# Two routing passes of a fused transformer kernel, each gathered into one stage on unnormalised tokens

## The chip, the cores and the metric

The kernel runs on one core of a Trainium2 chip. The metric is the device time of one execution in microseconds (us), lower is better. The core's engines are TensorE (PE, with its weight loads as PEld), VectorE (DVE), ScalarE (ACT), GpSimd (POOL) and the queue of SyncE (SP), which issues the transfers from HBM.

## The reference, cut to what matters

A sequence of 256 tokens with 1024 features passes through a first block (attention, a gated unit, cross attention, a mixture of experts) and through a second block of two layers, the last of which ends in another mixture. Everything is float32. Each mixture first normalises the tokens, then routes:

```
y = x * rsqrt(mean(x*x) + 1e-6) * g                 # g: one factor for each of the 1024 columns
# first mixture: 4 groups of 4 experts
glog = y @ w_rg + b_rg ; elog = y @ w_re + b_re     # 4 and 16 logits for each token
# best group by glog; best two experts of that group by elog; softmax over the two, times the group's probability
# second mixture: 8 experts
logits = y @ router                                  # best two, softmax over the two
# both: x += sum over the chosen experts of weight * (silu(y @ w_gate) * (y @ w_up)) @ w_down
```

## The kernel before

The program is a chain of stages. A stage is a block in which every engine has a program of its own, and no engine goes on to the next stage before all have ended. Weights come as pieces of 512 KB through a ring of 12 raw slots (`ring`). ScalarE writes the high part of a piece (`ring_hi`, L403, in the type float32r) and VectorE the low part (`ring_lo`, L408). SyncE loads a new piece into a slot when the piece that lay there has its low part. Each stage lets SyncE issue what fits (`issue_loads`).

The tokens `x` stand as rows, 128 on the partitions, in two halves (`[128, 2, 1024]`). `xT` is a pair (high, low) of turned tokens, `[128, 8, 256]`, with features on the partitions. Before each mixture these stages run:

- `clear_routing` (L2509 to L2517) loads the column factors as a row (`gain_row`) and clears `comb`, `chosen`, `place` and two banks of PSUM.
- `normed_T`, first stage: ScalarE squares and sums (L528), takes logarithm and exponential (L531, L533), VectorE multiplies the rows by `rinv` (L554).
- `normed_T`, second stage (`transposes`): TensorE turns the normalised rows in 16 steps (L480), ScalarE copies them times the column factors into the high part (L518, 8 instructions), VectorE makes the low part (L502, 8 instructions).
- `route`: TensorE multiplies the router, in plain float32, with both parts of `xT` (L1585, 8 steps in depth by 2 parts), ScalarE copies the sums (L1595), TensorE turns them back (L1590). Meanwhile VectorE multiplies the rows by the column factors (L1604), for the first mixture ScalarE and VectorE split them (L3000, L2978). Then VectorE, in the program `finish`, picks experts and weights in a chain of small instructions that each wait for the last (L2980 to L2993, or L3064 and on), with two short steps on ScalarE in between (L3003, L3005).
- `place_tokens`: TensorE counts tokens of each expert (L2532 to L2536), VectorE copies the counts (L2542 to L2550). For the first mixture it also writes the matrices `dispatch` (L2552) and `return_p` (L2555).
- `first_gather`: the tokens of the first experts are collected by matmuls with `dispatch` (L1286, 8 groups of 4 matmuls); for the first mixture VectorE and ScalarE copy a group of 4 in turn (L1297).
- The stage of the experts. Its programs hold two branches (`either`): the sparse one if no expert has more than 64 tokens (first mixture) or 128 (second), else the dense one, which reads `xT`.

Of the kernel before, what the change touches and what calls it, by code (L numbers as in the profile page):

```python
# [19 lines left out]
F32 = mybir.dt.float32  # L20
F32R = mybir.dt.float32r
ALU = mybir.AluOpType
# [139 lines left out]
def build(nc, ctx, A, consts_dram, const_cols, out):  # L162
# [1067 lines left out]
    def stacked_experts(group, xn_split, disp, ret, tag):  # L1230
# [42 lines left out]
        def programs(st):  # L1273
# [27 lines left out]
            def first_gather():  # L1301

                g, h, l = (S(n) for n in ("first_gathered", "bank_copied_act", "bank_copied_dve"))
                with stage() as block:
# [214 lines left out]
    def routed_experts(xn, stacked=None):  # L1519

        place_tokens(N_EXP2 if routed[0] else N_EXP1, stacked)
# [3 lines left out]
        with ExitStack() as st:  # L1525
# [5 lines left out]
            else:  # L1531
                dense = programs(st)
                first_gather, *sparse = sparse_experts(group, xn, tag)(st)
            limit = SLOTS if stacked else P
            first_gather()
            with stage() as block:
# [10 lines left out]
                def _(e):  # L1547
                    either(e, sparse[0], dense[0])

                @block.scalar  # L1550
                def _(e):
                    either(e, sparse[1], dense[1])
# [3 lines left out]
                def _(e):  # L1556
                    either(e, sparse[2], dense[2])
# [15 lines left out]
    def route(w, n, finish):  # L1573

        done, summed, copied = S("router_ready"), S("router_summed"), S("router_copied")
        with ExitStack() as st:
            logits_T = tmp(st, "logits_T", [n, SEQ])
            with stage() as block:
                sync_stage(block)
# [13 lines left out]
                def copy_sums(e):  # L1593
# [3 lines left out]
                finish(block, done, copy_sums)  # L1597

    gain_loaded = S("gain_row_loaded")

    def scale_tokens(e, step, xn, gain_row, ready=None):

        e.wait_ge(gain_loaded.sem, gain_loaded.total)
        step(v.tensor_tensor(xn[:], xn[:], row_bc(gain_row[:], [HALVES]), ALU.mult), ready or S("dve_chain"))  # L1604
# [899 lines left out]
    def clear_routing(gain_row, src):  # L2504

        with stage() as block:
            @block.sync
            def _(sp):
                gain_loaded.inc(sp.dma_start(gain_row[:], src.partition_broadcast(P)), 16)  # L2509
                issue_loads(sp)  # L2510
            dve = S("dve_chain")

            @block.vector
            def _(e):
                for t in (comb, chosen, place):
                    last = v.memset(t[:], 0.0)
                v.memset(bank(3, 2), 0.0)  # L2517
                dve.inc(last)

    def place_tokens(n, stacked):  # L2520

        counted, dve = S("tokens_counted"), S("dve_chain")
        with ExitStack() as st:
            top = tmp(st, "top_count", [P, 1])
            with stage() as block:
# [13 lines left out]
                def _(e):  # L2539
                    step = make_step(e)  # L2540
                    e.wait_ge(counted.sem, counted.at(1))
# [3 lines left out]
                    if stacked:  # L2545
# [408 lines left out]
    with ExitStack() as st:  # L2954
        xn = tmp(st, "xn_rows", [P, HALVES, D])
# [288 lines left out]
```

## Time and profile before

| | |
|---|---|
| median of 3 runs | 2504.54 us (2499.8 to 2505.14) |
| the profiled execution's own time | 2508.09 us |
| its span in the trace | 2506.3 us |
| busy PE / PEld | 2270.1 us (91%) / 1858.2 us (74%) |
| busy DVE / ACT / POOL | 1867.1 us (74%) / 1528.3 us (61%) / 50.5 us (2%) |
| mean granted TensorE clock | 0.941 |
| moved by DMA | 593.81 MB, 237 GB/s over the span |

The busy shares are means over stages with different limits. The two mixtures take most of the span: the experts of the first from 315 us on, those of the second from 1455 us on. The routing that the change touches lies just before each, at 267 to 315 us and at 1416 to 1455 us.

### The profile page before, as it was taken

Reading aid. Unit: us, or ns where it says so; the run is one execution under the profiler, and the core shown is the slowest. Engines: PE = TensorE matmul, PEld = TensorE weight load, DVE = VectorE, ACT = ScalarE, POOL = GpSimd, SP = SyncE. Lnnn points to the kernel's source line nnn. Section 1 sums busy time; section 2 is a strip of 40 time slices with the busy share of each in tenths; the row PEclk is TensorE's granted clock in tenths of the full one; section 3 lists DMA queues with packets and bytes.
Section 4 is the critical chain, followed back from the end, with each engine's and each line's share of the span. In section 5 each row is a group of like instructions: output and inputs, shape, how many; then the busy total and the mean of one; then the engine's idle time right before and its main releaser. Section 6 shows DMA issues by size and latency. Waiting matters only on the chain. (4 is left out here: it accounts for less than half of the span.)

```text
span 2506.3 us, 36936 instructions
## 1 busy us (share of the span) xinstructions
PE 2270.1 (91%) x11988; PEld 1858.2 (74%) x11988; DVE 1867.1 (74%) x2075; ACT 1528.3 (61%) x1997; POOL 50.5 (2%) x61
## 2 busy tenths in 40 slices
PE   7988589998987699988986689999999999999997
PEld 6777467776765599976765478888888888888885
DVE  4655588886755645545766569999999999999995
ACT  4554288886532344435532358787878787878784
POOL 0000000000001100000003000000000000000000
PEclk9989799999987899998987789999999999999998
DMA  8433099996630066644620079999999999999991
GB/s 297 134 128 107 9 373 361 353 342 239 188 101 1 22 219 185 186 148 143 179 67 2 30 251 376 336 372 336 377 334 371 336 375 335 374 335 374 336 375 67
DMA packets 280552, 593.81 MB, mean 237 GB/s; under 512 B 26208, under 2 KB 39424, under 8 KB 280320
## 3 DMA queue, kind: packets, MB, share of 16 engines
q1 hardware_dynamic: 280448, 592.45, 66.6%
q8 instruction: 62, 1.02, 0.2%
q14 instruction: 42, 0.34, 0.0%
HBM read 591.32 MB, written 1.05 MB: 236 GB/s over the span
## 5 line engine op out<-in xcount | busy, mean ns | idle before, releaser
L408 DVE TENSOR_TENSOR ring_lo<-ring,ring_hi 128x1024 fp32r<-128x1024 f32 (+1 forms) x1120 | 1337.9, 1215 | 306.8 <-ACT ring_hi L403 249.7
L403 ACT ACTIVATE ring_hi<-ring 128x1024 fp32r<-128x1024 f32 (+1 forms) x1120 | 1162.2, 1053 | 486.0 <-PE psum L426 432.7
L424 PE MATMUL psum<-ring_hi,xg_hi 128*128 128x512 f32 x896 | 356.2, 398 | 5.9 <-PEq L189 3.5
L426 PE MATMUL psum<-ring_hi,xg_lo 128*128 128x512 f32 x896 | 351.0, 392 | 0.0
L425 PE MATMUL psum<-ring_lo,xg_hi 128*128 128x512 f32 x896 | 350.3, 391 | 0.0
L424 PE MATMUL psum<-ring_hi,xT_hi 128*128 128x512 f32 (+2 forms) x512 | 201.5, 394 | 19.2 <-DVE ring_lo L408 10.3
L424 PEld LDWEIGHTS psum<-ring_hi,xg_hi 128*128 128x128 f32 x896 | 169.4, 189 | 40.0 <-issue 3.7
L426 PE MATMUL psum<-ring_hi,xT_lo 128*128 128x512 f32 (+2 forms) x512 | 197.8, 386 | 0.0
L425 PE MATMUL psum<-ring_lo,xT_hi 128*128 128x512 f32 (+2 forms) x512 | 197.7, 386 | 0.0
L426 PEld LDWEIGHTS psum<-ring_hi,xg_lo 128*128 128x128 f32 x896 | 169.1, 189 | 36.3
L425 PEld LDWEIGHTS psum<-ring_lo,xg_hi 128*128 128x128 f32 x896 | 169.6, 189 | 33.9
L424 PE MATMUL psum<-ring_hi,hT_hi 128*128 128x512 f32 x448 | 176.3, 394 | 8.8 <-DVE x L1210 5.2
L425 PE MATMUL psum<-ring_lo,hT_hi 128*128 128x512 f32 x448 | 175.1, 391 | 0.0
L426 PE MATMUL psum<-ring_hi,hT_lo 128*128 128x512 f32 x448 | 175.1, 391 | 0.0
L424 PE MATMUL psum<-xT_hi,ring_hi 128*128 128x256 f32 x480 | 137.2, 286 | 3.2 <-PEq L189 3.2
L425 PE MATMUL psum<-xT_lo,ring_hi 128*128 128x256 f32 x480 | 137.0, 285 | 0.0
L426 PE MATMUL psum<-xT_hi,ring_lo 128*128 128x256 f32 x480 | 136.9, 285 | 0.0
L424 PEld LDWEIGHTS psum<-ring_hi,xT_hi 128*128 128x128 f32 x512 | 98.8, 193 | 40.7 <-DVE ring_lo L408 9.4
L1327 PE MATMUL psum<-ring_hi,xg 128*128 128x512 f32 x256 | 108.8, 425 | 5.8 <-DVE ring_lo L408 3.8
L426 PEld LDWEIGHTS psum<-ring_hi,xT_lo 128*128 128x128 f32 x512 | 98.6, 192 | 19.6
L425 PEld LDWEIGHTS psum<-ring_lo,xT_hi 128*128 128x128 f32 x512 | 99.1, 194 | 18.3
L424 PEld LDWEIGHTS psum<-ring_hi,hT_hi 128*128 128x128 f32 x448 | 84.6, 189 | 29.5 <-issue 12.4
(501 smaller groups left out, 3242.8 us busy)
## 6 DMA issues: line engine op xcount, KB each, us to landing
ring<-in_moe_w_gate_dram SPq DMA_DIRECT2D x224, 512.0 KB, 5.3
ring<-in_moe_w_up_dram SPq DMA_DIRECT2D x224, 512.0 KB, 5.5
ring<-in_moe_w_down_dram SPq DMA_DIRECT2D x224, 512.0 KB, 4.9
ring<-in_w_in_dram SPq DMA_DIRECT2D x76, 512.0 KB, 5.1
ring<-in_w_gate_dram SPq DMA_DIRECT2D x64, 512.0 KB, 5.0
ring<-in_w_up_dram SPq DMA_DIRECT2D x64, 512.0 KB, 5.6
ring<-in_w_down_dram SPq DMA_DIRECT2D x64, 512.0 KB, 5.4
ring<-in_ffn_w_gate_dram SPq DMA_DIRECT2D x28, 512.0 KB, 3.7
```

Source lines behind the costliest of these rows:

```text
L403: sc.activation(raw_view(ring_hi, FINE, num, a, width), raw_view(ring, RAW, num, a, width), ACT.Copy) \
L408: v.tensor_tensor(raw_view(ring_lo, FINE, num, a, width), raw_view(ring, RAW, num, a, width), raw_view(ring_hi, FINE, num, a, width).bitca ...
L424: pe.matmul(out_, lhsT[0], rhs[0], start=start, stop=False)
L425: pe.matmul(out_, lhsT[0], rhs[1], start=False, stop=False)
L426: return pe.matmul(out_, lhsT[1], rhs[0], start=False, stop=stop)
L1327: pe.matmul(to, lhsT, w[0], start=start, stop=False)
```

## The change

The four stages `clear_routing`, both of `normed_T` and `route` become one stage, in both mixtures. TensorE turns the raw tokens. The router's rows are multiplied by the column factors (in place) and split in high and low parts, so the product is four float32r matmuls for each of the 8 steps in depth. The factor `rinv` of each token is applied to the logits instead. VectorE makes the normalised rows for the gather with one instruction for each half. ScalarE's sums of squares come behind its copies of the turned tokens. For the first mixture the high part of the rows is copied at the end of ScalarE's program, the low part (`meanwhile`) is made in `place_tokens`, and `return_p` is written in `first_gather`, where ScalarE now makes all eight copies. `xT` no longer holds normalised tokens, so the dense branches turn and split them first.

```diff
     def first_gather():                      # first mixture
                     @block.vector
                     def _(e):
-                        for k in range(0, KT, 2):
-                            e.wait_ge(g.sem, g.at(k + 1))
-                            l.inc(copy_gathered(v.tensor_copy, k, 0, bank(k)))
+                        for half in range(HALVES):
+                            for c in range(2):
+                                l.inc(v.tensor_tensor(ret[:, half, :, c * SLOTS:(c + 1) * SLOTS], disp[:, half, :, :].bitcast(F32),
+                                                      last_bc(comb[:, half, 1:E + 1], SLOTS), ALU.mult))
                     @block.scalar
                     def _(e):
-                        for k in range(1, KT, 2):
+                        for k in range(KT):
...
+            def all_tensor(e):               # dense branch alone; scalar and vector likewise
+                for i, part in enumerate(rows):
+                    for b in range(4):
+                        for m in range(4):
+                            k, h = 2 * b + m // 2, m % 2
+                            last = pe.transpose(bank(4 * i + b)[:, m * P:(m + 1) * P], part[:, h, k * P:(k + 1) * P], ident)
+                        last.then_inc(turned_n, 1)
+                e.wait_ge(split_n, 8)
+                dense[0](e)
...
-                    either(e, sparse[0], dense[0])
+                    either(e, sparse[0], all_tensor)
...
-    def route(w, n, finish):
+    def route(gain, row, w, n, xn, finish):
...
+        where = (0, 1, 5, 6)
+                @block.sync
+                def _(sp):
+                    gain_loaded.inc(sp.dma_start(gain_row[:], row.partition_broadcast(P)), 16)
+                    issue_loads(sp)
                 @block.tensor
                 def _(e):
+                    for b in range(4):
+                        for m in range(4):
+                            k, h = 2 * b + m // 2, m % 2
+                            last = pe.transpose(bank(where[b])[:, m * P:(m + 1) * P], x[:, h, k * P:(k + 1) * P], ident)
+                        turned_x.inc(last)
+                    e.wait_ge(w_lo.sem, w_lo.at(1))
                     for k in range(KT):
-                        for m, part in enumerate(xT):
-                            last = pe.matmul(bank(2)[0:n, 0:SEQ], w[:, k, :], part[:, k, :].bitcast(F32),
-                                             start=(k == 0 and m == 0), stop=(k == KT - 1 and m == 1))
+                        if k % 2 == 0:
+                            e.wait_ge(x_lo.sem, x_lo.at(k // 2 + 1))
+                        for i, w_ in enumerate(w_split):
+                            for j, x_ in enumerate(xT):
+                                last = pe.matmul(bank(2)[0:n, 0:SEQ], w_[:, k, :], x_[:, k, :], start=(k == 0 and i == 0 and j == 0),
+                                                 stop=(k == KT - 1 and i == 1 and j == 1))
...
+                def scalar_first(e):
+                    e.wait_ge(w_scaled.sem, w_scaled.at(1))
+                    w_hi.inc(sc.copy(w_split[0][:], w[:]))
+                    for b in range(4):
+                        e.wait_ge(turned_x.sem, turned_x.at(b + 1))
+                        x_hi.inc(sc.copy(pair_of(xT[0], b), bank(where[b])))
+                    use_table(LOG_EXP)
+                    for h in range(HALVES):
+                        sq.inc(sc.activation(junk[:, h, :], x[:, h, :], ACT.Square, accum_out=ss[:, h:h + 1]))
+                    e.wait_ge(sq.sem, sq.at(HALVES))
+                    act.inc(sc.activation(rms[:], ss[:], ACT.Ln, scale=1.0 / D, bias=eps))
+                    e.wait_ge(act.sem, act.total)
+                    rms_done.inc(sc.activation(rinv[:], rms[:], ACT.Exp, scale=-0.5))
                     e.wait_ge(summed.sem, summed.at(1))
                     copied.inc(sc.copy(logits_T[:], bank(2)[0:n, 0:SEQ]))
+                def vector_first(e, ready):
+                    w_scaled.inc(v.tensor_tensor(w[:], w[:], last_bc(gain[:], n), ALU.mult))
+                    for t in (comb, chosen, place):
+                        dve.inc(v.memset(t[:], 0.0))
+                    dve.inc(v.memset(bank(3, 2), 0.0))
+                    e.wait_ge(w_hi.sem, w_hi.at(1))
+                    w_lo.inc(v.tensor_tensor(w_split[1][:], w[:], w_split[0][:].bitcast(F32), ALU.subtract))
+                    for b in range(4):
+                        e.wait_ge(x_hi.sem, x_hi.at(b + 1))
+                        x_lo.inc(v.tensor_tensor(pair_of(xT[1], b), bank(where[b]), pair_of(xT[0], b).bitcast(F32), ALU.subtract))
+                    e.wait_ge(rms_done.sem, rms_done.at(1))
+                    e.wait_ge(gain_loaded.sem, gain_loaded.total)
+                    for h in range(HALVES):
+                        ready.inc(v.scalar_tensor_tensor(out=xn[:, h, :], in0=x[:, h, :], scalar=rinv[:, h:h + 1], in1=gain_row[:],
+                                                         op0=ALU.mult, op1=ALU.mult))
+                    e.wait_ge(done.sem, done.at(1))
...
-    def clear_routing(gain_row, src):
...
     def place_tokens(n, stacked, meanwhile):
                     step = make_step(e)
+                    meanwhile(step)
                     e.wait_ge(counted.sem, counted.at(1))
...
-                            for c in range(2):
-                                dve.inc(v.tensor_tensor(ret[:, h, :, c * SLOTS:(c + 1) * SLOTS], disp[:, h, :, :].bitcast(F32),
-                                                        last_bc(comb[:, h, 1:n + 1], SLOTS), ALU.mult))
...
     # finish of the first mixture
-                scale_tokens(e, step, xn, gain_row, xn_scaled)
-                e.wait_ge(xn_hi.sem, xn_hi.at(1))
-                step(v.tensor_tensor(xn_split[1][:], xn[:], xn_split[0][:].bitcast(F32), ALU.subtract))
-                e.wait_ge(done.sem, done.at(1))
-                step(v.tensor_tensor(gl[:], logits_psum[:, :, 0:N_GROUPS], row_bc(b_rg[:], [HALVES]), ALU.add))
-                step(v.tensor_tensor(el[:], logits_psum[:, :, N_GROUPS:N_GROUPS + N_EXP1], row_bc(b_re[:], [HALVES]), ALU.add))
+            vector_first(e, xn_ready)
+            for h in range(HALVES):
+                dve.inc(v.scalar_tensor_tensor(out=gl[:, h, :], in0=logits_psum[:, h, 0:N_GROUPS], scalar=rinv[:, h:h + 1],
+                                               in1=b_rg[:], op0=ALU.mult, op1=ALU.add))
+                dve.inc(v.scalar_tensor_tensor(out=el[:, h, :], in0=logits_psum[:, h, N_GROUPS:N_GROUPS + N_EXP1],
+                                               scalar=rinv[:, h:h + 1], in1=b_re[:], op0=ALU.mult, op1=ALU.add))
+            e.wait_ge(dve.sem, dve.total)
...
+            scalar_first(e)
...
+            e.wait_ge(xn_ready.sem, xn_ready.at(HALVES))
+            xn_hi.inc(sc.copy(xn_split[0][:], xn[:]))
...
+    def low_tokens(step):
+        step(v.tensor_tensor(xn_split[1][:], xn[:], xn_split[0][:].bitcast(F32), ALU.subtract))
+    routed_experts(xn_split, (disp1, ret1), low_tokens, routing.close)
...
     # finish of the second mixture
-                        step(v.tensor_copy(lg[:], logits_psum[:, :, 0:N_EXP2]))
+                        for h in range(HALVES):
+                            dve.inc(v.tensor_scalar(lg[:, h, :], logits_psum[:, h, 0:N_EXP2], rinv[:, h:h + 1], None, ALU.mult))
+                        e.wait_ge(dve.sem, dve.total)
```

## Rows read from the trace of the kernel before

**Rows 1.** Stretches: start:end, length, busy PE PEld DVE ACT POOL, PEclk, DMA share, GB/s

```profile
315.00:570.00 255.00, 250.02 (x1147) 183.85 (x1148) 223.03 (x227) 216.47 (x291) 0.00 (x0) 0.99 0.97 361
...
1455.00:2320.00 865.00, 856.23 (x3951) 709.95 (x3952) 796.29 (x733) 673.87 (x700) 0.00 (x0) 0.99 0.97 354
```

**Rows 2.** Timeline of SyncE's queue around both routings (start us, us, then what)

```profile
267.73 0.34 SPq L2509 DMA_DIRECT2D gain_row<-in_g_moe_row_dram  x1
314.87 2.54 SPq L397 DMA_DIRECT2D ring<-in_w_gate_dram  x4
...
1415.98 0.34 SPq L2509 DMA_DIRECT2D gain_row<-in_norm_ffn_row_dram  x1
1455.63 2.51 SPq L397 DMA_DIRECT2D ring<-in_moe_w_gate_dram  x4
```

**Rows 3.** Timeline of the first routing, up to the logits (in brackets: idle before)

```profile
266.17 1.29 DVE L624 TENSOR_TENSOR x<-x,psum 128x512 f32<-128x512 f32 x2 [1.88 <-PE psum L426]
...
269.40 1.06 ACT L528 ACTIVATE xn_rows<-x 128x1024 f32<-128x1024 f32 x1 [7.55 <-PEq L189]
...
271.94 0.20 ACT L533 ACTIVATE rinv<-rms 128x2 f32<-128x2 f32 x1
...
273.92 3.60 PE L480 MATMUL psum<-consts,xn_rows 128*128 128x128 f32 x16 [7.79 <-PEq L189]
...
288.41 0.36 ACT L1595 COPY logits_T<-psum 20x256 f32<-20x256 f32 x1 [4.57 <-PE psum L1585]
...
289.23 0.17 DVE L2980 TENSOR_TENSOR gl<-psum,r_b_rg 128x8 f32<-128x8 f32 x1 [2.99 <-PE psum L1590]
```

**Rows 4.** The router's matmuls in both routings: ns min/median/max, first and last start

```profile
L1585 PE MATMUL psum<-xT_hi,router x32: 376/379/634, 279.6 to 1435.7; 128*20 128x256 f32 x16, 128*8 128x256 f32 x16
```

**Rows 5.** Timeline: a 512-wide low part from PSUM; two neighbours of the gather

```profile
251.76 1.29 DVE L500 TENSOR_TENSOR cT_lo<-psum,cT_hi 128x512 fp32r<-128x512 f32 x2 [1.83 <-ACT cT_hi L518]
...
312.95 0.40 PE L1286 MATMUL psum<-dispatch,xn_moe_hi 128*128 128x256 f32 x2
...
313.19 0.40 PE L1286 MATMUL psum<-dispatch,xn_moe_lo 128*128 128x256 f32 x2
```

**Rows 6.** Groups by line in the first routing: busy us, mean ns | idle before

```profile
L2978 DVE TENSOR_TENSOR xn_moe_lo<-xn_rows,xn_moe_hi 128x2048 fp32r<-128x2048 f32 x1 | 2.3, 2292 | 2.0 <-ACT xn_moe_hi L3000 2.0
...
L3000 ACT CAST xn_moe_hi<-xn_rows 128x2048 fp32r<-128x2048 f32 x1 | 1.9, 1898 | 3.6 <-DVE xn_rows L1604 3.6
```

**Rows 7.** Stretches of the first routing, for the granted clock (columns as in group 1)

```profile
273.80:277.60 3.80, 3.60 (x16) 3.28 (x16) 1.69 (x4) 2.54 (x7) 0.00 (x0) 0.54 0.00 0
277.60:280.80 3.20, 1.18 (x6) 0.63 (x7) 2.88 (x6) 0.79 (x2) 0.00 (x0) 0.99 0.01 3
280.80:284.00 3.20, 3.20 (x9) 1.11 (x7) 1.16 (x2) 1.90 (x1) 0.00 (x0) 0.50 0.00 0
```

**Rows 8.** Timeline of the first mixture, from the logits to the experts

```profile
294.30 0.20 ACT L3005 ACTIVATE best<-best 128x2 f32<-128x2 f32 x1 [3.24 <-DVE best L1634]
...
296.43 0.19 DVE L2993 TENSOR_TENSOR chosen<-m,goh 128x32 f32<-128x32 f32 x1
...
299.49 0.19 DVE L2542 COPY place<-psum 128x32 f32<-128x32 f32 x1 [2.87 <-PE psum L2536]
...
300.55 1.22 DVE L2552 TENSOR_TENSOR dispatch<-consts,place 128x1024 fp32r<-128x1024 f32 x1
...
305.34 2.36 DVE L2555 TENSOR_TENSOR return_p<-dispatch,comb 128x1024 f32<-128x1024 f32 x2
...
313.62 0.59 ACT L1297 CAST xg<-psum 128x512 fp32r<-128x512 f32 x1 [0.37 <-PE psum L1286]
```

**Rows 9.** Timeline of the second routing: the first instruction on the logits

```profile
1437.35 0.17 DVE L3064 COPY lg<-psum 128x16 f32<-128x16 f32 x1 [7.14 <-PE psum L1590]
```

**Rows 10.** One instruction a step: dense feed-forward (L965), sparse experts (L1219)

```profile
L965 DVE TENSOR_TENSOR silu_gT<-silu_gT,psum x7: 1212/1214/1222, 907.3 to 1108.7; 128x1024 f32<-128x1024 f32 x7
...
L1219 DVE TENSOR_TENSOR hidden_rows<-silu_g,psum x56: 677/680/686, 1470.0 to 2444.8; 128x512 f32<-128x512 f32 x56
```

More of the change, by code:

```diff
@@ L1517, in expert_weight, with routed_experts @@
         return comb[:, h, slice(ex + 1, ex + 2) if isinstance(ex, int) else bass.ds(ex + 1, 1)]
-    def routed_experts(xn, stacked=None):
-        place_tokens(N_EXP2 if routed[0] else N_EXP1, stacked)
+    def routed_experts(xn, stacked=None, meanwhile=lambda step: None, placed=lambda: None):
+        place_tokens(N_EXP2 if routed[0] else N_EXP1, stacked, meanwhile)
+        placed()
         routed[0] += 1
@@ L1533, in routed_experts, with all_scalar, all_vector @@
                 first_gather, *sparse = sparse_experts(group, xn, tag)(st)
+            turned_n, split_n = (ctx.enter_context(nc.semaphore(n + tag)) for n in ("normed_turned", "normed_split"))
+            rows = [t[:].bitcast(F32) for t in xn] if stacked else [xn[:]]
+            pairs = [[t[:, 2 * b:2 * b + 2, :].rearrange("p k n -> p (k n)") for b in range(4)] for t in xT]
+            def all_tensor(e):
[7 more added lines that the diff above has]
+                dense[0](e)
+            def all_scalar(e):
+                for b in range(4):
+                    e.wait_ge(turned_n, b + 1)
+                    sc.copy(pairs[0][b], bank(b)).then_inc(split_n, 1)
+                dense[1](e)
+            def all_vector(e):
+                e.wait_ge(split_n, 4)
+                for b in range(4):
+                    if stacked:
+                        e.wait_ge(turned_n, 4 + b + 1)
+                        v.tensor_copy(pairs[1][b], bank(4 + b)).then_inc(split_n, 1)
+                    else:
+                        v.tensor_tensor(pairs[1][b], bank(b), pairs[0][b].bitcast(F32), ALU.subtract).then_inc(split_n, 1)
+                dense[2](e)
             limit = SLOTS if stacked else P
@@ L1547, in _ @@
                 def _(e):
-                    either(e, sparse[0], dense[0])
+                    either(e, sparse[0], all_tensor)
                 @block.scalar
                 def _(e):
-                    either(e, sparse[1], dense[1])
+                    either(e, sparse[1], all_scalar)
                     table[0] = LOG_EXP
@@ L1556, in _ @@
                 def _(e):
-                    either(e, sparse[2], dense[2])
+                    either(e, sparse[2], all_vector)
     def all_tokens_experts(combine):
@@ L1576, in route @@
         with ExitStack() as st:
             logits_T = tmp(st, "logits_T", [n, SEQ])
+            gain_row = tmp(st, "gain_row", [P, D])
+            junk = tmp(st, "x_squares", [P, HALVES, D])
+            ss, rms, rinv = (tmp(st, name, [P, HALVES]) for name in ("ss", "rms", "rinv"))
+            w_split = tmp_split(st, "router", [P, KT, n])
             with stage() as block:
-                sync_stage(block)
+                @block.sync
+                def _(sp):
+                    gain_loaded.inc(sp.dma_start(gain_row[:], row.partition_broadcast(P)), 16)
+                    issue_loads(sp)
@@ L1591, in _ @@
                     done.inc(last)
-                def copy_sums(e):
+                def scalar_first(e):
+                    e.wait_ge(w_scaled.sem, w_scaled.at(1))
+                    w_hi.inc(sc.copy(w_split[0][:], w[:]))
+                    for b in range(4):
+                        e.wait_ge(turned_x.sem, turned_x.at(b + 1))
[7 more added lines that the diff above has]
+                    rms_done.inc(sc.activation(rinv[:], rms[:], ACT.Exp, scale=-0.5))
@@ L1599, in build @@
+                finish(block, vector_first, scalar_first, rinv)
     gain_loaded = S("gain_row_loaded")
-    def scale_tokens(e, step, xn, gain_row, ready=None):
-        e.wait_ge(gain_loaded.sem, gain_loaded.total)
-        step(v.tensor_tensor(xn[:], xn[:], row_bc(gain_row[:], [HALVES]), ALU.mult), ready or S("dve_chain"))
     logits_psum = psum[:, 0:HALVES * BANK].rearrange("p (h c) -> p h c", h=HALVES)
@@ L2502, in build, with place_tokens @@
     largest = ctx.enter_context(nc.sbuf_tensor("largest_count", [P, 1], mybir.dt.int32))
-    def clear_routing(gain_row, src):
[L2506 to L2520, printed above, removed]
+    def place_tokens(n, stacked, meanwhile):
         counted, dve = S("tokens_counted"), S("dve_chain")
@@ L3008, in build @@
-    routed_experts(xn_split, (disp1, ret1))
+    routing = ExitStack()
+    xn = tmp(routing, "xn_rows", [P, HALVES, D])
+    gl, goh = tmp(routing, "gl", [P, HALVES, N_GROUPS]), tmp(routing, "goh", [P, HALVES, N_GROUPS])
+    ge = tmp(routing, "ge", [P, HALVES, N_GROUPS])
+    el = tmp(routing, "el", [P, HALVES, N_EXP1])
+    sel, c4, m4 = (tmp(routing, n, [P, HALVES, PER_GROUP]) for n in ("sel", "c4", "m4"))
+    gbest, gsum = tmp(routing, "gbest", [P, HALVES]), tmp(routing, "gsum", [P, HALVES])
```

96 lines of the change are left out of this document (42 added, 54 removed).

## The prediction

> **What bounds the kernel now.** I read the busy time by stretch first. In both loops of experts the share of the DMA engines is 0.97 and TensorE is busy nearly all the time [rows 1]; the reader is to see there that these loops run at a pace of their own, whatever happened before them. Then SyncE's queue: in the first routing it issues `gain_row` at 267.73 and nothing more until 314.87, in the second nothing between 1415.98 and 1455.63 [rows 2]. All 12 slots are full, so no weight moves. These two stretches, 47.1 and 39.7 us, are pure chain: each ends when its last stage ends, and the loop behind starts then. A microsecond taken out of the chain is a microsecond off the span. Last I read the timeline of the chain itself, engine by engine [rows 3, 8, 9].
>
> In what follows s is the time at which SyncE issues `gain_row`. From s to the first instruction on the logits the kernel takes 289.23 - 267.73 = 21.5 us in the first routing [rows 2, 3] and 1437.35 - 1415.98 = 21.4 us in the second [rows 2, 9]. A boundary between stages costs about 0.3 us (the last `x` addition ends at 267.46, s is 267.73 [rows 2, 3]).
>
> **The new first stage.** The four stages in a row become three lines that run side by side. I work out each from s.
>
> *VectorE, first part.* The old clearing stage lasts until ScalarE starts at 269.40, 1.67 us with one boundary, so the clearing is 1.4 [rows 2, 3]. The router's multiply and its low part have 160 elements for each partition in the first routing and 64 in the second; between 0.19 us for 32 elements [rows 8] and 2.29 for 2048 [rows 6] that is about 0.3 each. So the low parts of the tokens start at s + 2.1. Four of them, 512 wide from PSUM, cost 1.29 / 2 = 0.65 each [rows 5]: s + 4.7.
>
> *TensorE, transposes.* The 16 transposes took 3.60 us at a granted clock of 0.54, the lower level of 1.2 GHz [rows 3, 7]. At 2.4 GHz I take half, 1.9. Which level they get is not known. Before the change TensorE had idled 7.8 us in front of them [rows 3]; now it idles some 1.6. After a gap of about 2 us the router's matmuls began at 0.99 and fell to 0.50 a little over 1 us later [rows 7]. So both ends stay open.
>
> The Trainium skill ("TensorE: Matmul & The Clock Gate", Part 1) says that the low level is the default and that activity releases the clock. Read simply, that rule makes the shorter gap a gain, and both routings would take the faster end below, 2474.6 in all; the fall to 0.50 just behind 1.2 us of work shows that the trace does not follow so simple a reading.
>
> *ScalarE.* The router's high part is hidden behind the first transposes. A copy 512 wide from PSUM costs 0.59 [rows 8]. With fast transposes the four copies run back to back from s + 0.8 to s + 3.2; with slow ones the last ends 0.6 behind the last transpose, s + 4.3. Then come the sums of squares, logarithm and exponential, unchanged: 269.40 to 272.14, 2.74 us [rows 3]. `rinv` is there at s + 5.95 or s + 7.05.
>
> *VectorE, second part.* The rows for the gather now wait for `rinv`. The two instructions read two float32 tensors in SBUF; the nearest row is a difference of such tensors, 2.29 us for 2048 [rows 6] and 1.22 for 1024 [rows 8]. Two of them are 2.5 with the semaphore, so VectorE is free for the logits at s + 8.45 or s + 9.55.
>
> *TensorE, router.* 32 float32r matmuls of 256 columns. The gather's matmuls of that type and length start 0.24 us apart for two [rows 5], 0.12 each; 32 are 3.8 us at the upper level and 7.7 at the lower. From s + 2.8 with everything fast they would end at s + 6.6; from s + 3.7 with everything slow at s + 11.4. The old ones end just before the copy of the sums at 288.41, and the first logits instruction is at 289.23 [rows 3]: 0.85 behind the matmuls. So the logits stand ready between s + 7.5 and s + 12.3. With the clock up for part of them (the low stretch here was 3.2 us long [rows 7]) they are ready near s + 9.
>
> VectorE's line is thus the last one to end unless the clock stays low. I take the middle of its two ends, s + 9.0. Saved: 21.5 - 9.0 = 12.5 and 21.4 - 9.0 = 12.4. The bounds are s + 8.45 (13.0 saved) and s + 12.3 (9.2 saved).
>
> *The logits.* Two more small instructions in the first routing and one more in the second, some 0.1 each: -0.2 and -0.1. The chain behind is the same.
>
> **Behind the first stage, first mixture.** The high part of the rows, 1.90 us [rows 6], now follows the second exponential on ScalarE. That ends at 294.50 and VectorE's last instruction at 296.62 [rows 8]: 2.1 us of cover, so nothing, by a margin of 0.2. Without that cover it would be 1.9. The low part, 2.29 [rows 6], sits in `place_tokens` ahead of the counts. Nothing but the copy of the counts is queued behind it, and VectorE idled 2.87 us there [rows 8]; less the boundary of 0.3 that is 2.6. Also nothing, by 0.3; without cover 2.3.
>
> Taking `return_p` out: from 300.55 to 307.70 VectorE wrote two `dispatch` and four `return_p` of 1.22 each [rows 8]. Two remain, 2.5 us. Saved 7.15 - 2.5 = 4.7.
>
> In `first_gather` VectorE writes the four `return_p` in 4.9 us. ScalarE makes eight copies of 0.59, 4.7 us, from the first finished group on. The old stage ended with its copy at 314.21, 0.6 behind the last group [rows 8]. ScalarE is a little slower than the groups once the clock is up (four matmuls are 0.48), so it falls behind by some 0.5 at the end: -0.5, with bounds of 0 and -1. `return_p` is hidden behind that. In the second mixture these stages do not change.
>
> **Sum.** 12.5 - 0.2 + 12.4 - 0.1 + 4.7 - 0.5 = 28.8 us. The span goes from 2506.3 to 2477.5, the profiled execution's own 2508.09 to 2479.3. It stood 3.55 above the median of 2504.54, so the median comes to 2475.7. The fast ends give (13.0 + 13.0 - 0.3 + 4.7) 30.4 saved, 2474.1; with the gather's middle value 2474.6. The slow ends give 9.2 + 9.1 - 0.3 + 4.7 - 1 - 1.9 = 19.8, 2484.7. The runs before spread from 2499.8 to 2505.14, so I add 2.5 on either side: 2471.5 to 2487.
>
> The transposes and splits added to the dense branches cost nothing, as the trace shows the sparse ones taken in both mixtures (`dispatch` is used by L1286, and L1219 runs in all 56 steps [rows 5, 10]).
>
> **Rivals.**
>
> *The clock stays low in the new stage.* TensorE, not VectorE, then ends last, at s + 12.3, and the sum is 9.2 + 9.1 - 0.3 + 4.7 - 0.5 = 22.2 us, 2482.3. For it: transposes at 0.54 and half of the router's time at 0.50 [rows 7]. Against: the low stretch ended after 3.2 us of steady work, and here work is steady.
>
> *The narrow router does not run in one pass.* All float32r rows have 128 columns on the stationary side; the router has 20 or 8. If each of the 32 matmuls cost what a plain float32 one does (two records each, 32 for the 16 calls on the high parts; 16 calls in 8.8 us, less 1.6 for the low clock, 0.45 each [rows 3, 4, 7]), they take 14.4 us, the logits come at s + 18.1, and each routing saves 3.4 instead of 12.5. Sum 10.6, time 2493.9. Against it: 256 moving columns are the same as in the gather, and the moving side is what a matmul streams.
>
> *The gap is hidden anyway.* If the loops of experts were paced by transfers that could not start earlier, nothing would change: 2504. Against it: SyncE's first issue follows each last stage directly [rows 2].
>
> *Slower: the dense branch is taken.* The router's sums are rounded otherwise, and one expert of the second mixture could get over 128 tokens. A dense step takes (1108.7 - 907.3) / 6 = 33.6 us and a sparse one (2444.8 - 1470.0) / 55 = 17.7 [rows 10]; 56 steps at 15.9 more are 890 us, some 3366 in all. It decides from the 129th token on, and only if the count stands at that edge now; a last bit moves a token only where two logits nearly tie.
>
> **Chances.** My forecast 0.76, low clock 0.12, router in several passes 0.05, hidden 0.04, dense branch 0.03. The range leaves out the last three: 2470 to 2487. About 0.2%, 5 us, can be told from no change here. Faster takes the first three, 0.93; the same 0.04; slower 0.03.
>
> **What would show it.** In the new trace: the time from the issue of `gain_row` to the first `gl` or `lg` instruction, 9 us; the two instructions that write the rows just ahead of it; router matmuls 0.12 apart (one record each, 32 in a routing); VectorE free ahead of the counts; the last `dispatch` 2.5 us behind the first; the experts' loops as long as before. The prediction is wrong if the matmuls leave several records each, if VectorE waits for `logits_T` far behind s + 9, if ScalarE's high part ends behind the last choice, or if the loops of experts lengthen.

## The result, and the profile after

The changed kernel took 2470.66 us (median of 4 executions, 2468.57 to 2471.48) against 2504.84 for the kernel before (4 executions, 2499.8 to 2507.61): a ratio of 0.986, interval 0.9846 to 0.9873. The profiled execution took 2471.48 us, its span is 2469.7 and its mean granted clock 0.950 (0.941 before). Between the two profiled executions lie 36.6 us of span; the forecast was 28.8.

I cut the span at SyncE's first issue of each routing and at its next load of `ring`. First the kernel before, then the changed one, as stretches with the columns of group 1:

```profile
0.00:267.73 267.73, 227.17 (x1156) 189.77 (x1156) 151.39 (x204) 124.03 (x202) 1.16 (x5) 0.95 0.46 156
267.73:314.87 47.14, 20.51 (x92) 14.67 (x92) 27.12 (x66) 11.03 (x22) 0.00 (x0) 0.67 0.03 12
314.87:1415.98 1101.11, 976.12 (x5942) 789.86 (x5942) 730.62 (x888) 587.26 (x916) 49.30 (x56) 0.91 0.53 178
1415.98:1455.63 39.65, 21.08 (x92) 14.90 (x92) 13.98 (x41) 7.64 (x17) 0.00 (x0) 0.69 0.04 14
1455.63:2506.30 1050.67, 1025.27 (x4706) 849.02 (x4706) 943.97 (x876) 798.36 (x840) 0.00 (x0) 0.99 0.92 338
```

```profile
0.00:269.51 269.51, 229.48 (x1156) 191.41 (x1156) 151.44 (x204) 124.03 (x202) 1.16 (x5) 0.95 0.46 155
269.51:299.18 29.67, 14.18 (x92) 12.86 (x92) 22.83 (x61) 11.90 (x23) 0.00 (x0) 0.71 0.05 19
299.18:1393.92 1094.74, 969.92 (x5942) 785.66 (x5942) 730.82 (x888) 586.99 (x916) 49.45 (x56) 0.92 0.53 179
1393.92:1420.01 26.09, 14.45 (x92) 12.74 (x92) 12.07 (x39) 6.47 (x14) 0.00 (x0) 0.79 0.06 21
1420.01:2469.70 1049.69, 1023.22 (x4706) 847.70 (x4706) 943.73 (x876) 798.47 (x840) 0.00 (x0) 0.99 0.92 338
```

The reader is to see two things. The two routings are 17.47 and 13.56 us shorter, 31.0 together. The three stretches around them changed by +1.8, -6.4 and -1.0, -5.6 together, though TensorE executes the same number of instructions there; in the middle one its busy time fell by 6.2 and its granted clock rose from 0.91 to 0.92. The second difference needs an explanation of its own.

The timeline of the changed kernel's first routing up to the logits answers to [rows 3 to 5]; s is now 269.51:

```profile
269.51 0.34 SPq L1629 DMA_DIRECT2D gain_row<-in_g_moe_row_dram  x1
269.56 1.94 PE L1637 MATMUL psum<-consts,x 128*128 128x128 f32 x16 [1.64 <-PEq L189]
270.22 2.05 ACT L1658 CAST xT_hi<-psum 128x512 fp32r<-128x512 f32 x4
271.27 2.47 DVE L1678 TENSOR_TENSOR xT_lo<-psum,xT_hi 128x512 fp32r<-128x512 f32 x4
272.10 0.28 PE L1645 MATMUL psum<-xT_hi,router_hi 128*20 128x256 f32 x1 [0.60 <-DVE xT_lo L1678]
272.13 1.09 ACT L1661 ACTIVATE x_squares<-x 128x1024 f32<-128x1024 f32 x1
...
274.71 0.20 ACT L1665 ACTIVATE rinv<-rms 128x2 f32<-128x2 f32 x1
274.95 2.48 DVE L1682 SCALAR_TENSOR_TENSOR xn_rows<-x,rinv,gain_row 128x1024 f32<-128x1024 f32 x2 [1.21 <-ACT rinv L1665]
275.65 0.28 PE L1645 MATMUL psum<-xT_lo,router_lo 128*20 128x256 f32 x1
275.96 0.36 ACT L1667 COPY logits_T<-psum 20x256 f32<-20x256 f32 x1 [1.04 <-PE psum L1645]
277.35 0.22 DVE L3042 SCALAR_TENSOR_TENSOR gl<-psum,rinv,r_b_rg 128x4 f32<-128x4 f32 x1
```

The first instruction on the logits comes at s + 7.84, and in the second routing (s is 1393.92) at s + 7.84 again; I had said s + 9.0. The transposes and the first logits instruction there:

```profile
1393.97 1.94 PE L1637 MATMUL psum<-consts,x 128*128 128x128 f32 x16 [1.64 <-PEq L189]
1401.76 0.35 DVE L3129 TENSOR_SCALAR lg<-psum,rinv 128x8 f32<-128x8 f32 x2
```

In both, the first logits instruction shows no idle time in front of it: VectorE came straight from the two row instructions. Those had waited for `rinv`, 1.21 us in the first routing. The router's matmuls start 0.117 us apart, one record each, 32 in a routing.

The rest of that routing answers to [rows 8]:

```profile
282.77 1.88 ACT L3070 CAST xn_moe_hi<-xn_rows 128x2048 fp32r<-128x2048 f32 x1
284.82 0.19 DVE L3058 TENSOR_TENSOR chosen<-m,goh 128x32 f32<-128x32 f32 x1
285.56 2.29 DVE L3075 TENSOR_TENSOR xn_moe_lo<-xn_rows,xn_moe_hi 128x2048 fp32r<-128x2048 f32 x1 [0.54 <-PEq L189]
287.26 0.59 PE L2604 MATMUL psum<-chosen,consts 128*128 128x16 f32 x2
287.95 0.19 DVE L2611 COPY place<-psum 128x32 f32<-128x32 f32 x1
289.02 2.48 DVE L2621 TENSOR_TENSOR dispatch<-consts,place 128x1024 fp32r<-128x1024 f32 x2
292.03 4.63 DVE L1317 TENSOR_TENSOR return_p<-dispatch,comb 128x1024 f32<-128x1024 f32 x4 [0.53 <-PEq L189]
295.82 2.70 ACT L1297 CAST xg<-psum 128x512 fp32r<-128x512 f32 x5 [0.27 <-PE psum L1286]
299.18 0.40 SPq L397 DMA_DIRECT2D ring<-in_w_gate_dram  x1
```

Both halves of the split hide as forecast: ScalarE's ends at 284.65, 0.36 before VectorE's last choice; VectorE's ends at 287.85, together with the last counting matmul. `return_p` lies under the gather. The gather's matmuls, first in the kernel before, then in the changed one, as stretches:

```profile
307.90:313.70 5.80, 5.57 (x32) 5.40 (x32) 2.63 (x4) 1.84 (x4) 0.00 (x0) 0.69 0.01 3
291.90:297.90 6.00, 5.83 (x32) 5.66 (x32) 4.63 (x4) 3.78 (x7) 0.00 (x0) 0.65 0.01 4
```

They take 5.57 and 5.83 us, and the last copy ends 0.62 and 0.66 us behind them. So ScalarE, now alone with the copies, does not fall behind; the gather is longer because its matmuls are, at a granted clock of 0.65 instead of 0.69.

### The profile page after: what moved, and what is told of

Read it like the earlier page. It is cut to its first block and busy times, and to the rows that moved or that the text cites. A ratio compares the mean times of both kernels' runs of the same rounds, so it can differ in the third digit from the quotient of the medians.

```text
span 2469.7 us, 36864 instructions
## 1 busy us (share of the span) xinstructions
PE 2251.2 (91%) x11988; PEld 1850.4 (75%) x11988; DVE 1860.9 (75%) x2068; ACT 1527.8 (62%) x1995; POOL 50.6 (2%) x61
```

## The experiments

**Theories.** R: the change is worth what the two routings show, 31 us, and each part its own share; what the profiled executions show elsewhere is where TensorE's low clock happens to fall in the attention mixers. B, the rival: the later stages are faster by the code itself, by some 5 us, in every execution. Inside the first stage: VectorE's line (`rinv`, then the rows) sets its end, against TensorE's router.

The expectations use other letters. In first_only and second_only, A says that the low clock falls where the kernel's own timing puts it (so the gain in the mixers comes back), and B that it falls by chance. In same_again and after_delay1, P is the place of the low clock and C the code itself, which is B above.

The runs came in three sets, each compared on one chip with executions of the kernel before (medians 2502.68 of 8, 2507.95 of 9, 2506.47 of 17). Experiment kernels have other line numbers.

**first_only and second_only.** The new routing for one mixture alone, the old stages for the other (`return_p` goes with the first).

```diff
-    route(g_ffn2[layer], A["norm_ffn_2_row"][layer], router2, N_EXP2, xn, finish)
+    route_old(router2, N_EXP2, finish_old)      # first_only; second_only: the same for router1
```

> The new routing in the first mixture alone (return_p moved as well), the second as before. Theory A, the routing saves its chain in each mixture (17.5 and 13.5 us in the profiles) and the rest of the gain is TensorE's granted clock in the first layer's mixers (122.0 us long before, 116.1 after), which depends on when the work in front of them ends: first routing 29.7 us, mixers near 116, second routing 39.6, in all 21 to 24 us faster than before. Theory B, the rest is the spread between executions: mixers anywhere between 116 and 122, 17.5 us faster. My prediction's sum for this part was 16.5.

> The new routing in the second mixture alone. Up to 1416 us the work and its times are those of the kernel before. Theory A: first mixers stay at 122 us, the whole is 13.5 us faster and no more. Theory B, the rest of the gain is the spread: mixers vary as in any run. If the gain came from where the code lies, the mixers could change here too, since code behind them is shorter. My prediction's sum for this part was 12.3.

Measured: 2489.73 us (ratio 0.9942, interval 0.9923 to 0.996) and 2489.55 us (0.994, 0.9921 to 0.996), 13.0 and 13.1 below the kernel before. In first_only the routings are 29.60 and 39.50 us long, in second_only 47.12 and 26.16. Each mixture keeps its own gain, to 0.15 us, whichever way the other is done; the savings of 17.5 and 13.5 add up to the 31.0. The total of first_only falls short of its 17.5, though its interval (10 to 19 us) holds it; it does not hold the 21 to 24 of theory A. Nor did the gain in the mixers come back: the part of the mixer that took 68.93 us before and 64.52 after took 69.02 in first_only and 68.86 in second_only.

**return_only.** The old routings, with `return_p` written in `first_gather`.

```diff
-                            for c in range(2):      # place_tokens
-                                dve.inc(v.tensor_tensor(ret[:, h, :, c * SLOTS:(c + 1) * SLOTS], ...
+                        for c in range(2):          # first_gather, for each half
+                            l.inc(v.tensor_tensor(ret[:, half, :, c * SLOTS:(c + 1) * SLOTS], ...
```

> The kernel before with one part of the change alone: return_p is written in first_gather and no longer in place_tokens, ScalarE makes all eight copies there. By the itemised difference (-4.67 in the stage of the counts, +0.30 in the gather) the first routing goes from 47.1 to 42.8 us, the second stays at 39.6. Theory of the routings: time 4.3 us below the kernel before, with 2 or 3 us either way from where the low clock falls in the mixers. Rival (return_p only moves): first_gather waits for VectorE's four writes, 4.9 us, and the gain is under 1 us.

Measured: 2501.23 us (12 executions; ratio 0.9979, 0.997 to 0.9988), first routing 43.08 us. The part is worth 4.06 us in the stretch (4.3 were expected) and 5.2 in the total, whose interval of 3 to 7.5 us holds it, so the rest of the change is worth 13.4 there, much as in the second routing, which lacks this part.

**plain_router.** The router stays in plain float32: 16 calls instead of 32.

```diff
-                        for i, w_ in enumerate(w_split):
-                            for j, x_ in enumerate(xT):
-                                last = pe.matmul(bank(2)[0:n, 0:SEQ], w_[:, k, :], x_[:, k, :], ...
+                        for m, part in enumerate(xT):
+                            last = pe.matmul(bank(2)[0:n, 0:SEQ], w[:, k, :], part[:, k, :].bitcast(F32), ...
```

> As the changed kernel, but the 32 float32r matmuls of the split router are 16 plain float32 ones (the split is still made; the output stays the reference's). The matmuls then take 16 x 0.43 = 6.9 us instead of 32 x 0.117 = 3.75. If TensorE's line follows VectorE's by less than 1 us as in the trace after (logits turned back at 7.2 us, VectorE free at 7.8), the first instruction on the logits comes about 2.5 us later in each routing, 5 us in all against the changed kernel. A rival, that VectorE hides it: under 1 us. If the transposes' clock decides, the matmuls may fall to the lower level and it is 5 to 8.

Measured: 2478.09 us (ratio 0.9902, 0.9883 to 0.9922); routings 32.59 and 28.92, 2.9 and 2.8 longer than after. Two neighbours of its timeline, two records each, and the first logits instruction (s is 268.10):

```profile
271.12 0.59 PE L1671 MATMUL psum<-xT_lo,router 128*20 128x256 f32 x2
271.55 0.59 PE L1671 MATMUL psum<-xT_hi,router 128*20 128x256 f32 x2
...
278.54 0.22 DVE L3129 SCALAR_TENSOR_TENSOR gl<-psum,rinv,r_b_rg 128x4 f32<-128x4 f32 x1 [2.52 <-PE psum L1681]
```

A call takes 0.43 us against 4 x 0.117 = 0.47 for the four float32r matmuls that stand for two calls. So splitting the router makes its product 1.8 times as fast, and without it VectorE idles 2.52 us for TensorE and the logits come at s + 10.44. The split is worth 2.60 and 2.34 us in the two first stages, and 2.9 and 2.8 in the routings; in the second, most of the difference is the gather behind, 6.56 us against 6.05.

**long_gap.** ScalarE's squares, logarithm and exponential come first, and TensorE waits for `rinv` before it turns the tokens.

```diff
+                    e.wait_ge(rms_done.sem, rms_done.at(1))    # TensorE, ahead of the transposes
```

> As the changed kernel, but ScalarE makes squares, logarithm and exponential first and TensorE's transposes wait for the exponential, so TensorE idles about 4.4 us before them instead of 1.6. Theory of the short gap (the transposes run at 2.4 GHz since TensorE idled only 1.6 us): transposes fall to 3.6 us, and the router's matmuls start at the lower level; logits 3 us of order plus 2 to 4 us of clock later in each routing, 10 to 14 us in all. Rival, the clock in the new stage has nothing to do with the gap: transposes stay at 1.9 us, 6 us in all.

Measured: 2477.95 us (ratio 0.9901, 0.9882 to 0.9919); routings 33.17 and 29.88, 3.5 and 3.8 longer. The transposes, as a row of the timeline and as a stretch:

```profile
268.63 3.33 PE L1663 MATMUL psum<-consts,x 128*128 128x128 f32 x16 [5.03 <-ACT rinv L1694]
```

```profile
268.60:272.00 3.40, 3.37 (x18) 3.35 (x19) 1.38 (x2) 1.69 (x4) 0.00 (x0) 0.58 0.00 0
```

Behind an idle time of 5.03 us the 16 transposes take 3.33 us with the granted clock at 0.58, most of it the lower level of 1.2 GHz; behind 1.64 us in the changed kernel they take 1.94 at 1.00. In the second mixture they take 3.67 behind 4.85 us. The router behind them starts its matmuls 0.117 apart again, so the 10 to 14 us expected if it fell too did not come; the two routings lose 7.3. The first logits instruction (s is 265.19):

```profile
276.41 0.22 DVE L3129 SCALAR_TENSOR_TENSOR gl<-psum,rinv,r_b_rg 128x4 f32<-128x4 f32 x1 [0.63 <-PE psum L1681]
```

TensorE's line starts 3.39 us later and its transposes take 1.39 more, 4.8 in all, but the logits come at s + 11.22, only 3.38 later: part of the loss hides behind VectorE's rows, which ended last in the changed kernel. So the clock costs 1.4 us on TensorE's line; what it alone would cost the routing wasn't measured. Idle times between these weren't tried.

**same_again and same_third.** The changed kernel, nothing different, in two other sets.

> The changed kernel itself, beside kernels that are shifted. Theory P (the rest of the gain lies in the phase of TensorE's granted clock in the mixers, which falls as the work before happens to end): about 31 us faster than before from the two routings (17.5 and 13.5), plus what the phase gives, 0 to 5; in the profile the stretch from the first pair sums to the next load of p of the first layer again 64.5 us if the phase is fixed by the kernel's own timing, else up to 69. Theory C (the whole effect is one of code placement and stays): 34 us faster, 64.5 us again.

> The changed kernel once more, with nothing different. Theory that the excess over the two routings' 31 us comes from where TensorE's low clock falls in the mixers of each execution: the routings are 29.7 and 26.1 again, the time is anything from 2470 to 2478 and goes with the mean granted clock (about 10 us for 0.005), and the difference from the kernel before lies near 31 to 34 us. Rival, that the later stages gain some 5 us by the code itself: the median stays at 2470.7 within 1 us, 36 us below.

Measured: 2474.3 us (ratio 0.9874, 0.9854 to 0.9894) and 2474.01 us (0.9863, 0.9844 to 0.9883; single executions from 2464.37, with a mean granted clock of 0.952, to 2477.7, with 0.945). The stretches of same_third's profile:

```profile
0.00:267.33 267.33, 226.72 (x1156) 189.73 (x1156) 151.42 (x204) 124.05 (x202) 1.16 (x5) 0.95 0.46 156
267.33:297.01 29.68, 14.23 (x92) 12.88 (x92) 22.82 (x61) 11.91 (x23) 0.00 (x0) 0.71 0.06 19
297.01:1398.58 1101.57, 976.04 (x5942) 789.81 (x5942) 730.77 (x888) 587.52 (x916) 49.28 (x56) 0.91 0.53 178
1398.58:1424.66 26.08, 14.44 (x92) 12.76 (x92) 12.06 (x39) 6.47 (x14) 0.00 (x0) 0.79 0.07 21
1424.66:2475.10 1050.44, 1025.00 (x4706) 848.66 (x4706) 944.01 (x876) 798.81 (x840) 0.00 (x0) 0.99 0.92 338
```

The first routing repeats to 0.01 us in all three profiles of this code (29.67, 29.68, 29.68). The second took 26.09 and 26.08, but 25.29 in same_again. The difference lies in its gather; the gather's matmuls, in the changed kernel's first profile and in same_again:

```profile
1410.90:1417.00 6.10, 6.05 (x32) 5.86 (x32) 0.00 (x0) 0.00 (x0) 0.00 (x0) 0.61 0.00 0
1419.50:1424.90 5.40, 5.29 (x32) 5.10 (x32) 0.00 (x0) 0.03 (x1) 0.00 (x0) 0.71 0.00 0
```

So a difference of up to 0.8 us in a second routing can be the clock in its gather and not the code. In same_third the stretch between the routings is 1101.57 us, as long as in the kernel before (1101.11) and not as in the first profile of the same code (1094.74). That refutes B as the cause of the profiled difference. A part of the first block's mixer shows it most, the same instructions in the changed kernel's first profile and in same_third:

```profile
758.90:823.42 64.52, 42.74 (x614) 32.43 (x614) 44.94 (x54) 23.11 (x48) 21.84 (x25) 0.75 0.01 1
```

```profile
758.50:827.35 68.85, 46.40 (x614) 34.08 (x614) 44.83 (x54) 23.14 (x48) 21.64 (x25) 0.71 0.00 1
```

4.3 us of length go with 3.7 us of TensorE's busy time and a clock of 0.71 in place of 0.75; VectorE and ScalarE do the same in both. same_again lies between, 65.96 us at 0.72.

**after_delay1.** One more stage, a single VectorE clearing of two PSUM banks, ahead of the first gather: everything behind it comes later.

```diff
+            with stage() as block:
+                @block.vector
+                def _(e):
+                    late.inc(v.memset(bank(3, 2), 0.0))
```

> The changed kernel with one more small stage between the placing of the tokens and the first gather of the first mixture: one memset of 0.9 us, about 1.7 us with its boundary. Theory P: the first routing is 31.4 us, and the later stretches that run at the lower clock move: the pair-sum stretch comes out anywhere from 64 to 69 us, so the total is 1.7 us slower than the changed kernel plus or minus 4. Theory C: 1.7 us slower and 64.5 us.

Measured: 2476.2 us (ratio 0.988, 0.9859 to 0.9901), 1.9 above same_again of its set; first routing 31.97, 2.3 longer, where 1.7 was expected. The stage itself is 1.5 of that; the rest is the gather behind it, whose matmuls span 6.27 us from the first start to the last, against 5.43 after. In the total the shift cost no more than can be told. Two kernels with a longer delay, after_delay3 and, on the kernel before, before_delay3, gave no result, so a placement that always pays or always costs isn't excluded.

**rows_late and three_products.** In rows_late `rinv` no longer holds up VectorE: the rows get it in ScalarE's high part and in the low part (first mixture) or are made in `place_tokens` (second), and in the second the clearing of PSUM moves behind the low parts. three_products is rows_late without the product of the two low parts in the router.

```diff
+                        ready.inc(v.tensor_tensor(xn[:], x[:], row_bc(gain_row[:], [HALVES]), ALU.mult))
                         e.wait_ge(rms_done.sem, rms_done.at(1))
-                            ready.inc(v.scalar_tensor_tensor(out=xn[:, h, :], in0=x[:, h, :], scalar=rinv[:, h:h + 1], in1=gain_row[:], ...
...
-                            for j, x_ in enumerate(xT):
+                            for j, x_ in enumerate(xT[0:1] if i else xT):      # three_products
```

> The changed kernel, but rinv no longer holds up VectorE ahead of the logits. First mixture: VectorE multiplies the rows by the column factors while it waits for rinv, and rinv is applied later, in ScalarE's high part (two instructions) and in the low part (two instructions). Second mixture: the rows are made in the counting stage, where VectorE idles 2.85 us, and the 0.9 us of clearing PSUM moves behind the low parts. If VectorE's two row instructions set the end of the first stage (they end with the first logits instruction at s+7.84, while the turned logits were ready near s+7.2), the first logits instruction comes at s+7.2 in the first routing and, with the low parts 0.45 earlier, at s+6.75 in the second; two low parts of 1.28 in place of one of 2.29 cost 0.2 in the first. So -0.4 and -1.1, the two routings together 54.3 instead of 55.8 us. If TensorE's router set it as much, both stay at 29.7 and 26.1. The total can't show 1.5 us against the spread between executions; the stretches can.

> rows_late, and the router leaves out the product of the two low parts: 24 matmuls in place of 32. If TensorE's matmuls 0.117 us apart set the end of the stage once VectorE is out of the way, 8 fewer are 0.94 us: the second routing 0.9 shorter than in rows_late; in the first the multiplication by the column factors (2.29 us from s+4.25 on) takes over at s+6.6, so 0.6 shorter. Together some 52.8 us for both routings. If the split of the turned tokens (ScalarE's copies and VectorE's low parts) sets it, nothing changes against rows_late.

Measured: 2474.07 us (ratio 0.9871, 0.9854 to 0.9888) and 2471.54 us (0.9862, 0.9844 to 0.9881); routings 29.50 and 25.79, and 28.92 and 25.36. From the timelines of the first routing, rows_late (s is 269.54) and three_products (s is 268.18):

```profile
276.84 0.22 DVE L3144 SCALAR_TENSOR_TENSOR gl<-psum,rinv,r_b_rg 128x4 f32<-128x4 f32 x1 [0.87 <-PE psum L1682]
...
285.03 2.61 DVE L3184 SCALAR_TENSOR_TENSOR xn_moe_lo<-xn_rows,rinv,xn_moe_hi 128x1024 fp32r<-128x1024 f32 x2 [0.55 <-PEq L190]
```

```profile
274.54 0.22 DVE L3144 SCALAR_TENSOR_TENSOR gl<-psum,rinv,r_b_rg 128x4 f32<-128x4 f32 x1
```

With VectorE out of the way the logits come at s + 7.30, 0.54 earlier, and now TensorE is what VectorE waits for (0.87 us). Eight matmuls fewer bring s + 6.36, where VectorE shows no idle time again. So VectorE's rows were the last to end, as the prediction put it, but TensorE was only 0.5 behind. In the second routing they come at s + 6.95 and s + 6.14. So 1.4 us are taken out of the two first stages, or 3.2; 0.5 and 1.5 us reach the ends of the routings, where 1.5 and 3.0 were expected. In the first mixture the copy of the counts follows the last choice by 3.19 us in place of 2.94, because the two low parts take 2.61 in place of 2.29; and the gather's matmuls span 5.57 and 5.95 us from the first start to the last, against 5.43 to 5.46 in the three profiles of the changed kernel. In the second the two row instructions, 2.61 as well, outlast the counts, so that the copy of the counts follows the last weight by 3.19 us in place of 2.85. Its gather took 6.33 and 6.72 us, against 5.29 to 6.07 in the changed kernel; that is no more apart than two executions of one code, so what reaches the end of the second routing is known to some 0.8 us only. In the total neither can be told from the changed kernel (2474.01 in the same set).

The stretches of all profiled executions, in us. "Rest" is the span without the two routings; "loss" is its length times (1 - granted clock), summed over eleven stretches.

| | routing 1 | routing 2 | rest | loss in it |
|---|---|---|---|---|
| before | 47.14 | 39.65 | 2419.5 | 119.8 |
| after | 29.67 | 26.09 | 2413.9 | 110.9 |
| same_again | 29.68 | 25.29 | 2421.7 | 124.5 |
| same_third | 29.68 | 26.08 | 2419.3 | 119.1 |
| first_only | 29.60 | 39.50 | 2421.5 | 120.1 |
| second_only | 47.12 | 26.16 | 2416.8 | 113.6 |
| return_only | 43.08 | 39.63 | 2419.2 | 121.1 |
| plain_router | 32.59 | 28.92 | 2414.3 | 119.0 |
| long_gap | 33.17 | 29.88 | 2412.2 | 112.5 |
| after_delay1 | 31.97 | 26.17 | 2424.4 | 128.4 |
| rows_late | 29.50 | 25.79 | 2421.9 | 123.9 |
| three_products | 28.92 | 25.36 | 2417.9 | 120.5 |

The three rows of one kernel span 7.8 us in the rest, and the old and the partly changed kernels lie among them. The rest goes with the loss, though not exactly (plain_router is 3.6 to 7.2 us below the four rows with a loss from 119.1 to 120.5). What decides where the low clock falls in an execution isn't shown by these runs.

## Why the prediction came out as it did

The mechanism was right in the main and sizes were off: 2475.7 was forecast, with 2470 as the low end (the working gives 2471.5 and doesn't say why the range goes lower). The median of four is 2470.66, and the ratio of 0.986 times 2504.54 is 2469.5. Of the 6.2 us from the forecast to that, 2.2 are the routings, which saved 31.0 where 28.8 was said and 30.4 was the fast end. The other 4 are not in the stretches that the change touches; the ratios of the same code in the later sets, 0.9874 and 0.9863, would give 2473.0 and 2470.2, both above the low end. So 2.2 us come from a step that was mis-sized, and whether the range held was decided by the spread between executions.

*The step that failed* is the first logits instruction: "I take the middle of its two ends, s + 9.0", bound s + 8.45. It was s + 7.84 in both mixtures. Of the 1.16 us, 0.55 is the middle itself: the transposes ran at 1.00 and took 1.94, the faster of my two values (1.9). Another 0.55 is `rinv`, ready at s + 5.40 and not at s + 5.95. Behind that stands the sentence "the four copies run back to back from s + 0.8 to s + 3.2". I had spaced them by 0.59, the record of a single copy [rows 8]; in a row of four they took 2.05 us, starting 0.49 apart, and ended at s + 2.76, from s + 0.71, 0.44 earlier than I had them. The squares began 0.14 before the last copy's record ended. From the squares to `rinv` took 2.78 (forecast 2.74) and the two rows 2.48 (2.5); the last 0.06 lies in how these records join. Twice 1.16 is 2.3, nearly all of the 2.2 us by which the routings beat the sum; the other terms nearly cancel.

*The other terms.* First stages: 13.66 and 13.53 saved instead of 12.5 and 12.4. Logits: 0.27 and 0.19 lost (0.2 and 0.1). `return_p` out of `place_tokens`: 4.67 (4.7). Gather: 0.30 lost (0.5), but not by the reason given. ScalarE was to fall behind; it ended 0.66 us behind the last matmul, as against 0.62 before, and 0.26 of the 0.30 are the matmuls themselves, at a granted clock of 0.65 instead of 0.69. So that step had the wrong cause and a size that fits by luck. The boundaries in the first routing cost 0.29 more: 0.21 the one in front of the gather (0.53 us in place of 0.32), 0.07 the low part ahead of the counts, whose forecast cover of 0.3 was in fact gone. The second gather gave 0.24 by its clock. Router 0.117 apart: as taken.

*The clock.* I kept the low level open because of a fall to 0.50 in the old trace [rows 7]. The transposes began at full clock behind 1.64 us of idle time (after, both mixtures), and mostly at the low level behind 5.03 and 4.85 (long_gap) and 7.79 (before) [rows 3]. The rule of the Trainium skill ("TensorE: Matmul & The Clock Gate", Part 1), that the low level is the default and activity releases the clock, read simply, made the right choice here, the faster end; the trace after and long_gap agree with it by 1.94 against 3.33 us.

*The rest of the 36.6 us.* 5.6 us of the profiled difference lie outside the routings. They aren't a fixed gain of the code: same_third, the same code, has a rest of 2419.3 us, and the kernel before 2419.5. Whether a small part is, is open: over all executions taken (15 of the changed kernel, 38 of before) the means are 2472.9 and 2505.5, 32.6 us apart with a standard error of 1.2, so 1.6 +- 1.2 above the 31.0 of the routings (31.8 with same_again's second one); set by set the means are 33.9, 31.2 and 33.3 apart. The range had 2.5 us for the spread of single executions, taken from three of them (2499.8 to 2505.14); one kernel later spread over 13 (2464.37 to 2477.7).

*The rivals.* Low clock throughout: no, the stretches 269.50 to 276.80 and 1393.90 to 1400.60 have 1.00. Router in several passes: no, one record each. Hidden anyway: no, each loop starts behind its routing. Dense branch: no, TensorE executes as many instructions behind each routing as before (5942 and 4706), and the stretch with the second loop is as long (1050.67 and 1049.69).

## What to carry to other kernels

When stages of a serial stretch are laid side by side, work out each engine's line from a common start and take instructions in a row by their spacing, not by the duration of a single record. Each line that one shortens uncovers the next: here VectorE, then TensorE 0.5 us behind, and of 3.2 us that three_products took out of the first stages 1.5 arrived. Judge a gain of 1% by the stretch that the change touches, and profile one kernel more than once to learn how well that stretch repeats (0.01 us in the first routing here, 0.8 in the second); the total also holds where the low clock fell, and needs many executions.

## What the runs showed of the hardware

- ScalarE's copies of 128x512 from PSUM: 0.59 us as a single record, 2.05 us for four in a row, which start 0.49 apart (after).
- A float32r matmul with 20 or 8 stationary columns and 256 moving ones starts 0.117 us behind the last, as fast as with 128; the plain float32 one 0.43, in two records.
- 16 transposes: 1.94 us behind 1.64 us of idle time (after), 3.33 behind 5.03 (long_gap).
- The 32 matmuls of the second gather, the same code in two executions: 6.05 us at a granted clock of 0.61 (after), 5.29 at 0.71 (same_again).
- The same code, 614 matmuls of a mixer, took 64.52 us at a granted clock of 0.75 in one execution and 68.85 at 0.71 in another. Over the 92 executions of all these kernels whose clock is on record, with the routings of each kernel as in its profile, the span without the routings grew by 0.61 us for each microsecond of loss (its length times 1 - mean clock), correlation 0.81; over the 15 of the changed kernel alone by 0.69, correlation 0.92.
